# Gated delta rule on one core: the decay buffers doubled, the decay differences moved ahead in VectorE's order, and half of the block copies sent from ScalarE's queue

## The chip, the cores and the metric

The kernel runs on one core of one Trainium2 chip. The metric is the device time of one execution in microseconds (us). Three runs of the kernel before gave 2969.79 to 2971.79 us, with a median of 2971.08 us.

## The reference, cut to what matters

The model is two transformer-like blocks over 528 tokens (16 meta tokens and 512 others) with 1024 channels. Everything up to the delta rule and everything after it is unchanged by this edit; the edit lies in one stage of the first block, the gated delta rule, which is computed once forwards and once backwards in time for 8 heads of 128 channels.

```python
kk   = einsum("bnhid,bnhjd->bnhij", k, k)
decay = exp(where(tri, g[..., :, None] - g[..., None, :], -inf))
lmat = where(strict, beta[..., :, None] * kk * decay, 0.0)
a    = lmat + eye(CHUNK)
sol  = triangular_solve(a, concat(v * beta, k * beta * exp(g)))   # unit lower triangular
qk   = einsum("bnhid,bnhjd->bnhij", q, k) * decay
# then over the chunks, in order:
v_new = u_c - w_c @ S
o_c   = qd_c @ S + qk_c @ v_new
S     = S * exp(g_last) + kd_c.T @ v_new
```

Here `g` is the running sum of the log decays within a chunk, `qd` is q times exp(g), and S is the state that one chunk hands to the next. The outputs of both directions are added.

## The kernel before, in words

The stage cuts the 528 tokens into 5 chunks of C = 106 rows, and the 8 heads into 2 groups of 4. A step handles one chunk of 4 heads in both directions at once; there are STEPS = 10 steps. Direction u = 0 runs forwards and u = 1 backwards, and almost everything exists twice, once for each u. PSUM banks 0 to 3 belong to u = 0, and 4 to 7 to u = 1.

The order of the work is written out by hand, one function per engine: `pe_delta`, `act_delta`, `dve_delta`, `pool_delta` and `sp_delta`. Each has a loop over t that interleaves three steps in different phases. "Ahead" is step t: decays, k times k, and the inverses of the diagonal blocks. "Inner" is step t-1: the inverse is completed in three levels of matrix products. "Outer" is step t-2: solve, outputs and state. All engines run their own list in order, and wait on semaphores for what they need.

The pieces that the change touches or moves are these:

- `decay_diff(t)` on VectorE (DVE), L1423: differences of the summed decays, from the PSUM bank that TensorE (PE) filled in `spread_decay` (L1186), into the tile `dec`. ScalarE (ACT) takes their exponential in place in `exp_diff` (L1371).
- `decayed_qk(t-1)` on DVE, L1453: q times k times the previous step's `dec`, into `qkm`. Since there is one `dec` per direction, `decay_diff(t)` stands behind it, with a drain of DVE between them.
- `decayed_values(t-2)`, L1434, writes `rr`; PE's output products (`outputs`, L1263 and L1264) wait for it. `lower(t)`, L1444, then writes `mt`, the lower triangular matrix of the chunk.
- `exp_decay(t)` on ACT, L1366, writes `qd`, which has two buffers per direction; it waits until PE's outputs of step t-2 have read the buffer. GpSimd (POOL) multiplies it by q in L1314.
- `product_out` on ACT, L1376, copies a level's product from PSUM to `pp`. PE needs it for `level_update`, and DVE's `inverse_next` (L1474 and L1476) follows. The order on ACT is exp_diff, exp_decay, then product_out for levels 0, 1 and 2.
- The 16x16 diagonal blocks of `mt` are inverted on DVE (`block_begin`, L1494, and the functions after it). To bring 28 blocks of each direction into one layout, they go through DRAM: the sync engine's queue (SP) sends 7 small transfers for each direction into `block_in` (L1156, the "cuts"), waits until all 14 have landed, reads them back into `uu` and `raw` (L1159, L1160), later sends the inverted blocks out (L1163), and puts them into `xq` with 14 transfers (L1170, the "placements").
- DVE's order in one t is: rest, decayed_qk, drain, decay_diff, decayed_values, lower, add_output, inverse_next level 0, block_begin and the blocks up to size 4, state_next, inverse_next level 1, block 8 in two halves with inverse_next level 2 between them, block_turned.

After the last step SP goes on to load weights into `wraw` (L452), whose first half is the new room of one of the decay buffers.

Of the kernel before, what the change touches and what calls it, by code (L numbers as in the profile page):

```python
# [17 lines left out]
F32 = mybir.dt.float32  # L18
# [6 lines left out]
P = 128  # L25
# [125 lines left out]
def build_program(nc, io):  # L151
# [41 lines left out]
    eps = keep("eps", [P, 1])  # L193
    rstd = keep("rstd", [P, T])
# [37 lines left out]
    CB, PB = 4 * W4, 4 * GH * P  # L232
    free_h, free_l = stage_pos - 3 * 4 * DM, stage_pos - 4 * DM
    room = {"base": [base, base + KT * F], "b": [b_at, b_at + 2 * KT * F], "d": [d_at, nc.sbuf_usable_end],
            "stage": [stage_pos, stage_pos + 2 * F], "free_h": [free_h, free_h + 4 * DM],
            "free_l": [free_l, free_l + 4 * DM]}
# [11 lines left out]
    for u in range(2):  # L248
        d = {}
        d["kt"] = [dsb("base", f"kt{u}{v}", [C, GH * P]) for v in range(2)]  # L250
        d["vt"] = [dsb("b", f"vt{u}{v}", [C, GH * P]) for v in range(2)]
        d["state"] = dsb("base", f"state{u}", [P, GH * P])
        d["rr"] = dsb("stage", f"rr{u}", [C, GH * P])
        d["vn"] = dsb("d", f"vn{u}", [C, GH * P])
        d["xq"] = [dsb("b", f"xq{u}{v}", [C, 2 * W4]) for v in range(2)]
        d["qd"] = [dsb("d", f"qd{u}{v}", [P, W4]) for v in range(2)]
        d["qkm"] = [dsb("d", f"qkm{u}{v}", [C, W4]) for v in range(2)]
        d["mt"] = [dsb("b", f"mt{u}{v}", [C, W4]) for v in range(2)]
        d["dec"] = dsb("base", f"dec{u}", [C, W4])
# [114 lines left out]
    d_cut, d_in, d_y, d_yout = map(sem, ("blocks_cut", "blocks_in", "blocks_inverted", "blocks_out"))  # L374
# [767 lines left out]

    def sp_delta(sp):

        sp.wait_ge(d_y, 1)
        for u in range(2):
            sp.dma_start(scr_in[u], uu[0:LANES, :]).then_inc(d_cut, 16)
        sp.wait_ge(d_cut, 32)
        cells = [scr_in[u].rearrange("(r l) (a b) -> l a r b", l=NBLK, b=BASE) for u in range(2)]
        back = [scr_out[u].rearrange("w (r l) (a b) -> l a (w r) b", l=NBLK, b=BASE) for u in range(2)]  # L1150
        for n in range(STEPS):
            for u in range(2):
                sp.wait_ge(d_mt[u], n + 1)
                for bl in range(NBLK):
                    src, k = diagonal(delta[u]["mt"][n % 2], bl)
                    sp.dma_start(cells[u][bl, 0:k, :, 0:k], src).then_inc(d_cut, 16)  # L1156
            sp.wait_ge(d_cut, 32 + 32 * NBLK * (n + 1))
            sp.wait_ge(d_y, n + 1)
            sp.dma_start(uu[0:LANES, :], scr_in[0]).then_inc(d_in, 16)  # L1159
            sp.dma_start(raw[32:32 + LANES, :], scr_in[1]).then_inc(d_in, 16)  # L1160
            sp.wait_ge(d_y, n + 2)
            for u in range(2):
                sp.dma_start(scr_out[u].rearrange("w p n -> p w n"),  # L1163
                             yy[32 * u:32 * u + LANES, :].rearrange("p (w n) -> p w n", w=2)).then_inc(d_yout, 16)
            sp.wait_ge(d_yout, 32 * (n + 1))
            for u in range(2):
                sp.wait_ge(d_cleared[u], n + 1)
                for bl in range(NBLK):
                    dst, k = diagonal(delta[u]["xq"][n % 2], bl)
                    sp.dma_start(dst, back[u][bl, 0:k, :, 0:k]).then_inc(d_x0[u], 16)  # L1170

    def pe_delta(pe):
# [79 lines left out]
        def outputs(n, u):  # L1252
            d = delta[u]
            qd, qkm = d["qd"][n % 2], d["qkm"][n % 2]
# [47 lines left out]
    def pool_delta(pool):  # L1302
# [8 lines left out]
        def decay_q(n, u):  # L1311
            qd = heads4(delta[u]["qd"][n % 2], C)
            wait(pool, d_eg[u], n + 1)
            pool.tensor_tensor(qd, qd, columns4(n, u, 0), ALU.mult).then_inc(d_qd[u], 1)  # L1314
# [39 lines left out]
    def act_delta(act):  # L1354
# [8 lines left out]
        def exp_decay(n, u):  # L1363
            wait(act, d_darg[u], n + 1)
            wait(act, d_o[u], n - 1)
            act.activation(delta[u]["qd"][n % 2][:, :], ps[:, 4 * u + 2, 0:W4], ACT.Exp).then_inc(d_eg[u], 1)  # L1366

        def exp_diff(n, u):
            dec = delta[u]["dec"]
            wait(act, d_darg[u], n + 1)  # L1370
            act.activation(dec[:, :], dec[:, :], ACT.Exp).then_inc(d_dec[u], 1)  # L1371
# [19 lines left out]
        for t in range(STEPS + 2):  # L1391
# [4 lines left out]
            if t < STEPS:  # L1396
                each(exp_diff, t)
                each(exp_decay, t)
            if 1 <= t <= STEPS:
                for lv in range(L):  # L1400
                    each(product_out, t - 1, lv)

    def dve_delta(dve):
# [15 lines left out]
        def decay_diff(n, u):  # L1419
            d, cc, h = delta[u], chunk(n, u), head0(n)  # L1420
            wait(dve, d_gbc[u], n + 1)
            for r, sl in enumerate(head_slices(C)):
                last = dve.tensor_scalar(d["dec"][:, sl], ps[0:C, 4 * u + 2, sl],  # L1423
# [14 lines left out]
        def lower(n, u):  # L1438
# [4 lines left out]
            for r, sl in enumerate(head_slices(C)):  # L1443
                last = dve.scalar_tensor_tensor(d["mt"][n % 2][:, sl], ps[0:C, 4 * u + 1, sl],  # L1444
                                                tok_b[:, cc, h + r:h + r + 1], d["dec"][:, sl],
# [3 lines left out]
        def decayed_qk(n, u):  # L1449
# [3 lines left out]
            dve.tensor_tensor(d["qkm"][n % 2][:, :], ps[0:C, 4 * u, 0:W4], d["dec"][:, :], ALU.mult  # L1453
# [1384 lines left out]
```

## Time and profile before

| what | value |
|---|---|
| median of 3 runs | 2971.08 us |
| the profiled execution's own time | 2974.84 us |
| its span | 2973.1 us |
| PE busy | 2763.3 us (93%) |
| DVE busy | 1459.4 us (49%) |
| the delta rule's stretch | about 255 to 641 us |
| granted clock of PE over the span | 0.967 of full speed |

The span is what the trace covers. Shares over the whole span say little here, since the edit concerns the stretch of the delta rule alone. In a timeline row the number in brackets is the engine's idle time just before the row, and what ended it; "x8" means that eight instructions of one line were merged into the row. Starts are us from the start of the span. In a row of busy times the stretch comes first and then its length, and then what the group's line names.

### The profile page before, as it was taken

What the parts mean: (1) busy time and instruction counts of PE and PEld (TensorE: products, weight loads), DVE (VectorE), ACT (ScalarE), POOL (GpSimd) and SP (SyncE); (2) the same over time, 40 slices, a digit from 0 to 9 for tenths busy, and PEclk for the clock granted to TensorE, in tenths of its full rate; (3) what the DMA queues carried; (4) which work ended last, traced back from release to release, by engine and by line L of the source; (5) the groups of instructions that cost most, each with busy time, mean ns of one, the idle gap of its engine ahead of it and who ended that gap; (6) DMA issues with size and microseconds to landing.
All of it is one profiled execution on the core that took longest, in us unless ns stands there. A gap on an engine that the chain in (4) does not pass through costs nothing.

```text
span 2973.1 us, 48213 instructions
## 1 busy us (share of the span) xinstructions
PE 2763.3 (93%) x17591; PEld 2419.9 (81%) x17591; DVE 1459.4 (49%) x2316; ACT 1024.3 (34%) x1759; POOL 1096.7 (37%) x588
## 2 busy tenths in 40 slices
PE   6986888889999999999899789999999999999998
PEld 6964777868987778888679679999998988877876
DVE  2664676643221754233778555444366224555433
ACT  4761222223234242222423564222233255422221
POOL 3422333314434444444437103444443310244443
PEclk8997888889999999999999999999999999999999
DMA  2210000012233333333312002223322210123332
GB/s 95 91 49 7 10 10 10 10 40 85 92 92 92 92 94 92 97 94 92 92 43 65 8 1 68 88 88 90 92 85 79 66 35 1 57 85 99 92 92 92
DMA packets 88859, 197.90 MB, mean 67 GB/s; under 512 B 38140, under 2 KB 40238, under 8 KB 88728
## 3 DMA queue, kind: packets, MB, share of 16 engines
q1 hardware_dynamic: 84964, 192.72, 21.9%
q10 hardware_dynamic: 3764, 3.38, 0.4%
q8 instruction: 88, 1.44, 0.2%
q14 instruction: 43, 0.35, 0.0%
HBM read 192.24 MB, written 3.82 MB: 66 GB/s over the span
## 4 chain that ended last, share of the span: by engine, by line
issue 44%; PE 17%; POOL 12%; DVE 4%; ACT 1%; DVEq 1%; POOLq 1%; ACTq 0%
POOL wl L476 12%; PE ps L512 9%; PE ps L2151 2%; PE ps L2182 2%; DVE work L2051 1%; DVE top L2048 1%; PE ps L2169 1%; PE ps L1798 1%; PE ps L2301 1%; PE ps L2310 1%; ACT prob L2220 0%; POOLq L129 0%; DVE rowmax L2251 0%; PE ps L2154 0%; PE ps L887 0%
## 5 line engine op out<-in xcount | busy, mean ns | idle before, releaser
L476 POOL TENSOR_TENSOR wl<-wraw,wh 128x1024 fp32r<-128x1024 f32 x353 | 875.8, 2481 | 1293.0 <-ACT wh L468 1292.9
L468 ACT ACTIVATE wh<-wraw 128x1024 fp32r<-128x1024 f32 x353 | 372.5, 1055 | 578.4 <-PE ps L512 490.4
L512 PE MATMUL ps<-xah,wh 128*128 128x264 f32 (+1 forms) x2672 | 500.7, 328 | 23.4 <-ACT xah L841 14.2
L512 PE MATMUL ps<-xah,wl 128*128 128x264 f32 (+1 forms) x2672 | 488.3, 323 | 0.0
L512 PE MATMUL ps<-xal,wh 128*128 128x264 f32 (+1 forms) x2672 | 487.3, 322 | 0.0
L512 PEld LDWEIGHTS ps<-xah,wh 128*128 128x128 f32 x2672 | 406.0, 190 | 77.9 <-issue 23.4
L512 PEld LDWEIGHTS ps<-xah,wl 128*128 128x128 f32 x2672 | 403.9, 189 | 41.1 <-issue 0.5
L512 PEld LDWEIGHTS ps<-xal,wh 128*128 128x128 f32 x2672 | 402.8, 188 | 40.7
L660 DVE TENSOR_TENSOR res<-res,stage 128x512 f32 (+3 forms) x112 | 81.8, 730 | 440.1 <-ACT stage L576 440.1
L512 PE MATMUL ps<-xbh,wh 128*128 128x264 f32 (+1 forms) x1392 | 274.7, 337 | 13.4 <-POOL wl L476 12.8
L512 PE MATMUL ps<-xbh,wl 128*128 128x264 f32 (+1 forms) x1392 | 269.9, 334 | 0.0
L512 PE MATMUL ps<-xbl,wh 128*128 128x264 f32 (+1 forms) x1392 | 269.5, 333 | 0.0
L512 PEld LDWEIGHTS ps<-xbh,wh 128*128 128x128 f32 x1392 | 218.2, 189 | 48.1 <-POOL wl L476 16.4
L576 ACT ACTIVATE stage<-ps 128x512 f32<-128x512 f32 (+1 forms) x136 | 81.9, 602 | 467.3 <-PE ps L512 467.2
L512 PEld LDWEIGHTS ps<-xbh,wl 128*128 128x128 f32 x1392 | 217.9, 188 | 27.5
L512 PEld LDWEIGHTS ps<-xbl,wh 128*128 128x128 f32 x1392 | 217.5, 188 | 27.4
L653 DVE TENSOR_SCALAR xbh<-stage 128x512 f32 (+3 forms) x102 | 144.8, 1420 | 18.2 <-issue 16.6
L2151 PE MATMUL ps<-pf,qz 128*104 128x264 f32 (+4 forms) x384 | 124.0, 409 | 24.7 <-ACT prob L2220 13.8
L2251 DVE TENSOR_REDUCE rowmax<-ps 106x1 f32<-106x106 f32 (+4 forms) x160 | 77.7, 488 | 126.5 <-PE ps L2156 70.8
L655 DVE TENSOR_TENSOR xbl<-stage,xbh 128x512 f32 (+3 forms) x102 | 114.1, 1119 | 15.3 <-issue 1.3
L1178 PE MATMUL ps<-xq,ob 106*106 106x106 f32 x480 | 67.4, 309 | 51.7 <-DVE xq L1474 33.5
L1178 PEld LDWEIGHTS ps<-xq,ob 106*106 106x106 f32 x480 | 63.1, 221 | 53.6 <-DVE xq L1474 35.0
(332 smaller groups left out, 3277.7 us busy)
## 6 DMA issues: line engine op xcount, KB each, us to landing
wraw<-in_w SPq DMA_DIRECT2D x353, 512.0 KB, 3.5
res<-in_x SPq DMA_DIRECT2D x4, 528.0 KB, 5.5
res<-in_x ACTq DMA_DIRECT2D x1, 2048.0 KB, 7.8
out<-res SPq DMA_DIRECT2D x1, 2048.0 KB, 6.9
block_in<-mt SPq DMA_DIRECT2D x120, 4.0 KB
xq<-block_out SPq DMA_DIRECT2D x120, 8.0 KB
block_out<-yy SPq DMA_DIRECT2D x20, 56.0 KB
cossin<-in_cossin ACTq DMA_DIRECT2D x1, 528.0 KB
```

The source lines that it names most:

```text
L468: act.activation(wh[:, s * DM:(s + 1) * DM], wraw[:, s * DM:(s + 1) * DM], ACT.Copy).then_inc(hi_done, 1)
L476: pool.tensor_tensor(wl[:, s * DM:(s + 1) * DM], wraw[:, s * DM:(s + 1) * DM], wh[:, s * DM:(s + 1) * DM].bitcast(F32), ALU.subtract).then ...
L512: mm = pe.matmul(ps[:, 2 * s + h, 0:width], ws[:, s * DM + kk * P:s * DM + (kk + 1) * P], x[:, at:at + width], start=(h not in [o[0] for o ...
L576: act.activation(shaped(out(j, u), live), acc(b, live=live), func, **more).then_inc(acc_free, 1)
L653: dve.tensor_scalar(hi, x, 1.0, None, ALU.mult)
L655: return dve.tensor_tensor(lo, x, hi.bitcast(F32), ALU.subtract)
L660: return dve.tensor_tensor(r, r, live_stage(u) if live else stage_at(u), ALU.add)
L1178: mm = pe.matmul(out_[:, sl], lhs(r, sl), rhs(r, sl), start=True, stop=True)
L1798: mm = pe.matmul(ps[0:ROWS[t], 4 + 2 * (n % 2) + x, 0:c], ix_zero[:, 2 * (m % 2) + hh, C * t:ENDS[t]], pf[:, 16 * T + o:16 * T + o + c], s ...
L2151: pe.matmul(s, qz[:, 2 * (p % 2) + hh, t * C:ENDS[t]], pf[:, key + o:key + o + c], start=True, stop=False)
L2182: mm = pe.matmul(ps[0:rows, 7, t * 64:(t + 1) * 64], ptr[n % 2][0:ROWS[kb], kb * rows:(kb + 1) * rows], v[0:ROWS[kb], kb, col:col + 64], s ...
L2251: most = dve.tensor_reduce(m, psum_cols(plan["unit", n][0], rows, w_), AX.X if w_ <= 512 else AX.XY, ALU.max, negate=True)
```

## The change

Five edits go together. The tile `dec` gets two buffers per direction, used by n % 2. The tile `qd` gets three, used by n % 3, so that `exp_decay` waits for the outputs of step t-3 and not t-2. On DVE, `decay_diff(t)` is moved ahead of `decayed_qk(t-1)`, and the drain between them goes. The cuts of direction 1 are issued from ACT's queue, behind exp_decay and ahead of product_out. SP issues only those of direction 0, and waits for each direction by its own semaphore before it reads that direction back. Some small tiles change places (`uu`, `raw`), and SP waits at the end until the last `dec` has been read, since one buffer lies in the room for weights.

```diff
-        d["qd"] = [dsb("d", f"qd{u}{v}", [P, W4]) for v in range(2)]
+        d["qd"] = [dsb(("d", "d", ("rstd", "free_h")[u])[v], f"qd{u}{v}", [P, W4]) for v in range(3)]
-        d["dec"] = dsb("base", f"dec{u}", [C, W4])
+        d["dec"] = [dsb(("base", "free_raw")[v], f"dec{u}{v}", [C, W4]) for v in range(2)]
...
+    def cut_blocks(q, n, u):
+
+        cells = scr_in[u].rearrange("(r l) (a b) -> l a r b", l=NBLK, b=BASE)
+        q.wait_ge(d_mt[u], n + 1)
+        for bl in range(NBLK):
+            src, k = diagonal(delta[u]["mt"][n % 2], bl)
+            q.dma_start(cells[bl, 0:k, :, 0:k], src).then_inc(d_cut[u], 16)
...
         for n in range(STEPS):
+            cut_blocks(sp, n, 0)
             for u in range(2):
-                sp.wait_ge(d_mt[u], n + 1)
-                for bl in range(NBLK):
-                    src, k = diagonal(delta[u]["mt"][n % 2], bl)
-                    sp.dma_start(cells[u][bl, 0:k, :, 0:k], src).then_inc(d_cut, 16)
-            sp.wait_ge(d_cut, 32 + 32 * NBLK * (n + 1))
-            sp.wait_ge(d_y, n + 1)
-            sp.dma_start(uu[0:LANES, :], scr_in[0]).then_inc(d_in, 16)
-            sp.dma_start(raw[32:32 + LANES, :], scr_in[1]).then_inc(d_in, 16)
+                sp.wait_ge(d_cut[u], 16 + 16 * NBLK * (n + 1))
+                sp.wait_ge(d_y, n + 1)
+                blocks_of = (uu[0:LANES, :], raw[32:32 + LANES, :])[u]
+                sp.dma_start(blocks_of, scr_in[u]).then_inc(d_in, 16)
...
+        for u in range(2):
+            sp.wait_ge(d_qkd[u], STEPS)
...
         def exp_decay(n, u):
             wait(act, d_darg[u], n + 1)
-            wait(act, d_o[u], n - 1)
-            act.activation(delta[u]["qd"][n % 2][:, :], ps[:, 4 * u + 2, 0:W4], ACT.Exp).then_inc(d_eg[u], 1)
+            wait(act, d_o[u], n - 2)
+            act.activation(delta[u]["qd"][n % 3][:, :], ps[:, 4 * u + 2, 0:W4], ACT.Exp).then_inc(d_eg[u], 1)
...
                 each(exp_diff, t)
                 each(exp_decay, t)
+                act.wait_ge(d_cut[1], 16)
+                wait(act, d_in, 32 * t)
+                cut_blocks(act, t, 1)
...
             if outer:
                 each(rest, t - 2)
+            if ahead:
+                each(decay_diff, t)
             if inner:
                 each(decayed_qk, t - 1)
-            if ahead:
-                dve.drain()
-                each(decay_diff, t)
             if outer:
                 each(decayed_values, t - 2)
```

On DVE, in loop turn t = 4, the kernel before has this order (the numbers behind a tile's name tell buffers apart; rr is the rest and then the decayed values, mt the lower matrix):

```order
198 L1414 SCALAR_TENSOR_TENSOR rr_107<-ps,tok_neg,vt_104 106x128 x4
199 L1414 SCALAR_TENSOR_TENSOR rr_124<-ps,tok_neg,vt_121 106x128 x4
200 L1453 TENSOR_TENSOR qkm_114<-ps,dec_117 106x424
201 L1453 TENSOR_TENSOR qkm_131<-ps,dec_134 106x424
202 L1423 TENSOR_SCALAR dec_117<-ps,tok_cum 106x106 x4
203 L1423 TENSOR_SCALAR dec_134<-ps,tok_cum 106x106 x4
204 L1434 TENSOR_SCALAR rr_107<-ps,tok_bk 106x128 x4
205 L1434 TENSOR_SCALAR rr_124<-ps,tok_bk 106x128 x4
```

And the changed kernel, at the same place:

```order
198 L1427 SCALAR_TENSOR_TENSOR rr_107<-ps,tok_neg,vt_104 106x128 x4
199 L1427 SCALAR_TENSOR_TENSOR rr_126<-ps,tok_neg,vt_123 106x128 x4
200 L1436 TENSOR_SCALAR dec_118<-ps,tok_cum 106x106 x4
201 L1436 TENSOR_SCALAR dec_137<-ps,tok_cum 106x106 x4
202 L1466 TENSOR_TENSOR qkm_115<-ps,dec_119 106x424
203 L1466 TENSOR_TENSOR qkm_134<-ps,dec_138 106x424
204 L1447 TENSOR_SCALAR rr_107<-ps,tok_bk 106x128 x4
205 L1447 TENSOR_SCALAR rr_126<-ps,tok_bk 106x128 x4
```

The eight differences have moved ahead of the two qkm products, and write another buffer than the one that the products read. Row numbers are places in DVE's list; lines of the changed kernel are 13 higher here.

On ACT, a loop turn of the kernel before reads as follows, from the new values to level 1:

```order
121 L1383 ACTIVATE vn_108<-ps,tok_b 106x128 x4
122 L1383 ACTIVATE vn_125<-ps,tok_b 106x128 x4
123 L1371 ACTIVATE dec_117<-dec_117 106x424
124 L1371 ACTIVATE dec_134<-dec_134 106x424
125 L1366 ACTIVATE qd_111<-ps 128x424
126 L1366 ACTIVATE qd_128<-ps 128x424
127 L1376 ACTIVATE pp_118<-ps 106x424
128 L1376 ACTIVATE pp_135<-ps 106x424
```

In the changed kernel, a loop turn reads:

```order
161 L1393 ACTIVATE vn_108<-ps,tok_b 106x128 x4
162 L1393 ACTIVATE vn_127<-ps,tok_b 106x128 x4
163 L1381 ACTIVATE dec_118<-dec_118 106x424
164 L1381 ACTIVATE dec_137<-dec_137 106x424
165 L1376 ACTIVATE qd_112<-ps 128x424
166 L1376 ACTIVATE qd_131<-ps 128x424
167 L1152 DMA block_in<-mt_135 16x4x16 x6
168 L1152 DMA block_in<-mt_135 10x4x10
169 L1386 ACTIVATE pp_120<-ps 106x424
170 L1386 ACTIVATE pp_139<-ps 106x424
```

Seven transfers now stand between exp_decay and the first product_out.

## Rows read from the trace of the kernel before

**Rows 1.** PE, PEld, DVE, ACT, POOL busy (instructions), PE clock, DMA share, GB/s.

```profile
255.00:641.00 386.00, 313.50 (x2504) 296.20 (x2504) 251.81 (x714) 94.95 (x220) 130.85 (x140) 0.86 0.07 11
```

**Rows 2.** Waits of DVE, 255 to 641 us: total, times, longest.

```profile
DVE qkm L1453 <- PE ps L1178: 25.2, 9, 3.3
DVE uu L1494 <- DMA raw<-block_in: 21.8, 9, 7.8
```

**Rows 3.** Timeline of DVE in loop turn t = 5.

```profile
427.63 1.35 DVE L1453 TENSOR_TENSOR qkm<-ps,dec 106x424 f32<-106x424 f32 x2 [2.75 <-PE ps L1178]
429.07 1.98 DVE L1423 TENSOR_SCALAR dec<-ps,tok_cum 106x106 f32<-106x106 f32 x8
430.96 2.15 DVE L1434 TENSOR_SCALAR rr<-ps,tok_bk 106x128 f32<-106x128 f32 x8
433.03 1.97 DVE L1444 SCALAR_TENSOR_TENSOR mt<-ps,tok_b,dec 106x106 f32<-106x106 f32 x8
442.28 0.60 DVE L1476 TENSOR_TENSOR xq<-xq,ps 106x424 f32<-106x424 f32 x1
444.18 0.37 DVE L1494 COPY uu<-raw 28x256 f32<-28x256 f32 x1 [1.30 <-DMA raw<-block_in]
```

**Rows 4.** Timeline of DVE in t = 10, where no differences are due.

```profile
610.23 1.34 DVE L1453 TENSOR_TENSOR qkm<-ps,dec 106x424 f32<-106x424 f32 x2 [2.02 <-PE ps L1178]
611.49 2.15 DVE L1434 TENSOR_SCALAR rr<-ps,tok_bk 106x128 f32<-106x128 f32 x8
```

**Rows 5.** Timeline of SP's queue in t = 5.

```profile
434.09 7.03 SPq L1156 DMA_DIRECT2D block_in<-mt  x14
442.42 0.40 SPq L1160 DMA_DIRECT2D raw<-block_in  x1
```

**Rows 6.** Transfers issued from ACT's queue at the kernel's start.

```profile
0.76 0.44 ACTq L2551 DMA_DIRECT2D gains<-in_gains  x1
5.50 1.40 ACTq L2553 DMA_DIRECT2D sel<-in_sel  x1
```

**Rows 7.** ACT's first product_out of t = 2, 5 and 8.

```profile
322.12 0.52 ACT L1376 ACTIVATE pp<-ps 106x424 f32<-106x424 f32 x1 [0.85 <-PE ps L1178]
...
438.43 0.52 ACT L1376 ACTIVATE pp<-ps 106x424 f32<-106x424 f32 x1 [0.16 <-PE ps L1178]
...
546.28 0.52 ACT L1376 ACTIVATE pp<-ps 106x424 f32<-106x424 f32 x1 [0.16 <-PE ps L1178]
```

**Rows 8.** DVE's lower in t = 2, 6 and 8, block copy in 6 and 8.

```profile
319.00 1.97 DVE L1444 SCALAR_TENSOR_TENSOR mt<-ps,tok_b,dec 106x106 f32<-106x106 f32 x8
...
468.68 1.97 DVE L1444 SCALAR_TENSOR_TENSOR mt<-ps,tok_b,dec 106x106 f32<-106x106 f32 x8
...
478.93 0.67 DVE L1494 COPY uu<-raw 28x256 f32<-28x256 f32 x1 [2.58 <-DMA raw<-block_in]
...
539.35 1.97 DVE L1444 SCALAR_TENSOR_TENSOR mt<-ps,tok_b,dec 106x106 f32<-106x106 f32 x8
...
550.83 0.37 DVE L1494 COPY uu<-raw 28x256 f32<-28x256 f32 x1
```

**Rows 9.** PE's first output products in t = 5 and t = 6.

```profile
432.23 0.44 PE L1263 MATMUL ps<-qd,state 128*128 128x106 f32 x2 [2.40 <-DVE rr L1434]
...
467.39 0.39 PE L1263 MATMUL ps<-qd,state 128*128 128x106 f32 x2
```

**Rows 10.** Busy times in t = 5 and t = 6 beside these products.

```profile
432.50:435.50 3.00, 3.00 (x17) 3.00 (x16) 2.50 (x11) 0.00 (x0) 1.20 (x2) 0.51 0.04 7
467.50:470.50 3.00, 3.00 (x29) 3.00 (x28) 3.00 (x14) 1.64 (x3) 3.00 (x4) 1.00 0.16 17
```

**Rows 11.** One block product on DVE at t = 0 and t = 4, and POOL beside the latter.

```profile
272.61 0.43 DVE L1512 TENSOR_TENSOR tmp<-uu,yy 60x64 f32<-60x64 f32 x2
...
409.73 1.26 DVE L1512 TENSOR_TENSOR tmp<-uu,yy 60x64 f32<-60x64 f32 x2
409.08 1.79 POOL L1307 TENSOR_TENSOR mt<-scum,sel 16x424 f32<-16x424 f32 x2
```

More of the change, by code:

```diff
@@ L193, in build_program @@
     eps = keep("eps", [P, 1])
+    rstd_at = keep.pos[0]
     rstd = keep("rstd", [P, T])
@@ L255, in build_program @@
         d["xq"] = [dsb("b", f"xq{u}{v}", [C, 2 * W4]) for v in range(2)]
-        d["qd"] = [dsb("d", f"qd{u}{v}", [P, W4]) for v in range(2)]
+        d["qd"] = [dsb(("d", "d", ("rstd", "free_h")[u])[v], f"qd{u}{v}", [P, W4]) for v in range(3)]
         d["qkm"] = [dsb("d", f"qkm{u}{v}", [C, W4]) for v in range(2)]
         d["mt"] = [dsb("b", f"mt{u}{v}", [C, W4]) for v in range(2)]
-        d["dec"] = dsb("base", f"dec{u}", [C, W4])
+        d["dec"] = [dsb(("base", "free_raw")[v], f"dec{u}{v}", [C, W4]) for v in range(2)]
         d["pp"] = dsb("b", f"pp{u}", [C, W4])
         delta.append(d)
-    uu, raw, yy = (dsb("free_h", name, [64, n * BASE * BASE]) for name, n in (("uu", 1), ("raw", 1), ("yy", 2)))
+    uu, yy = dsb("base", "uu", [64, BASE * BASE]), dsb("free_h", "yy", [64, 2 * BASE * BASE])
+    raw = place("raw", [64, BASE * BASE], F32, room["free_l"][0])
     tmp, half = dsb("free_l", "tmp", [64, 2 * BASE * BASE]), dsb("free_l", "half", [64, BASE * BASE // 4])
@@ L373, in build_program @@
     d_cleared = both("inverse_cleared")
-    d_cut, d_in, d_y, d_yout = map(sem, ("blocks_cut", "blocks_in", "blocks_inverted", "blocks_out"))
+    d_cut = both("blocks_cut")
+    d_in, d_y, d_yout = map(sem, ("blocks_in", "blocks_inverted", "blocks_out"))
     d_ks, d_rr, d_xr, d_vn, d_vk, d_o, d_oa, d_ds, d_st = map(both, (
@@ L1170, in sp_delta @@
                     sp.dma_start(dst, back[u][bl, 0:k, :, 0:k]).then_inc(d_x0[u], 16)
+        for u in range(2):
+            sp.wait_ge(d_qkd[u], STEPS)
     def pe_delta(pe):
@@ L1253, in outputs @@
             d = delta[u]
-            qd, qkm = d["qd"][n % 2], d["qkm"][n % 2]
+            qd, qkm = d["qd"][n % 3], d["qkm"][n % 2]
             wait(pe, d_qd[u], n + 1)
@@ L1311, in decay_q @@
         def decay_q(n, u):
-            qd = heads4(delta[u]["qd"][n % 2], C)
+            qd = heads4(delta[u]["qd"][n % 3], C)
             wait(pool, d_eg[u], n + 1)
@@ L1422, in decay_diff @@
             for r, sl in enumerate(head_slices(C)):
-                last = dve.tensor_scalar(d["dec"][:, sl], ps[0:C, 4 * u + 2, sl],
+                last = dve.tensor_scalar(d["dec"][n % 2][:, sl], ps[0:C, 4 * u + 2, sl],
                                          tok_cum[:, u, cc, h + r:h + r + 1], 0.0, ALU.subtract, ALU.min)
@@ L1452, in decayed_qk @@
             wait(dve, d_o[u], n - 1)
-            dve.tensor_tensor(d["qkm"][n % 2][:, :], ps[0:C, 4 * u, 0:W4], d["dec"][:, :], ALU.mult
+            dve.tensor_tensor(d["qkm"][n % 2][:, :], ps[0:C, 4 * u, 0:W4], d["dec"][n % 2][:, :], ALU.mult
                               ).then_inc(d_qkd[u], 1)
```

15 lines of the change are left out of this document (7 added, 8 removed).

## The prediction

> **What bounds the kernel now.** First read the busy times by stretch: the edit lies in the 386.00 us of the delta rule, where PE is busy 313.50 us and DVE 251.81 [rows 1]. Neither is full, so here a cycle of waits sets the pace. The second view is DVE's waits. Two of them are those that the edit aims at: 25.2 us in front of qkm for PE's products, and 21.8 us in front of the block inversion for the blocks on their way through DRAM [rows 2]. The third view is the timeline of one loop turn. In t = 5 DVE idles 2.75 us before L1453, although the decay differences that come right behind it need only a PSUM bank filled before the solve; they take 1.98 us and delay the decayed values, which PE's outputs wait for, and `lower` [rows 3]. PE stands idle 2.40 us for those values [rows 9]. From `lower`'s start, called L (433.03), it goes on two ways that meet at the block copy: DVE's own level-0 updates end at 442.88 = L+9.85, and the blocks arrive at 444.18 = L+11.15, after 1.30 us of idling [rows 3]. From the block copy to the next `lower`, DVE's list has hardly a gap except the one before qkm. A turn takes some 37 us, and what is saved in one is saved in the time, since DVE's list runs through all of them.
>
> **Part 1: differences first.** Before, qkm to decayed values is 430.96 - 427.63 = 3.33 us start to start [rows 3]. At t = 10, where no differences are due, the same distance is 611.49 - 610.23 = 1.26 us [rows 4]. The difference, 2.07 us, goes from the path, provided the eight differences fit in the idle time before qkm. That is 2.75 us here against 1.98 us of work [rows 3]. The nine waits before qkm total 25.2 us; one of them is t = 10 with 2.02 [rows 2, 4], so the eight of t = 2 to 9 average 2.9 us. At t = 1 there is none and nothing is gained. 8 x 2.07 = 16.6 us. Next in line is POOL's masking of qkm, about 1 us for each direction behind the product, which ends before PE's second half of the outputs; I add nothing for it.
>
> **Part 2: the cuts from two queues.** SP issues 14 cuts in 7.03 us, and `raw` is issued 442.42 - 441.12 = 1.30 us after that [rows 5]. In the new order SP sends 7 from L+1.06, and ACT 7 from L+1.97, when the second `mt` is ready. An issue on ACT's queue held it 0.44 us at the start of the kernel [rows 6], about 0.47 with its spacing, so ACT's last ends near L+5.3; `raw` would be issued at about L+6.6 and be in SBUF 1.76 us later (444.18 - 442.42 [rows 3, 5]), at L+8.4. The blocks are then no longer late: DVE's level-0 updates are, at L+9.85. So each wait in front of the block copy can be won down to the 0.1 us that separates any two DVE instructions here, but no further.
>
> What hides ACT's seven issues? They stand ahead of product_out, which in t = 5 starts at 438.43 = L+5.40 [rows 7]: just the time at which the issues end (L+5.3). The cover is full with 0.1 us to spare. In t = 2 it is not: product_out starts at 322.12 = L+3.12, L being 319.00, so it would be pushed by 2.2 us; PE does both directions' products before the first update, which forgives 0.6, and 1.6 us are lost [rows 7, 8]. exp_decay, which stood before product_out and waited for the outputs, is out of the way, but PE had product_out's input hardly earlier, so I count nothing for the third `qd` buffer.
>
> The sum of part 2: waits of 21.8 us, of which the longest, 7.8, is t = 0, leave 14.0 us in eight turns of t = 1 to 9; t = 8 has none [rows 2, 8]. Off go 8 x 0.1 = 0.8, the 1.6 of t = 2, some 0.3 for smaller pushes of product_out, and 2.2 at t = 6. There no decayed values are due, so PE's outputs start at 467.39, before `lower` at 468.68 [rows 8, 9]: the updates don't get earlier with `lower`, and part 1 and part 2 together can win only the 2.58 us of idling there less 0.3, not 2.1 + 2.5. That leaves 9.1 us. At t = 0 nothing but the transfers is due: the last issue from ACT ends 1.9 us before SP's did, which is 1.9 us. Together 11.0 us.
>
> **Part 3: PE's clock.** In t = 5 PE comes out of 2.40 us of idling [rows 9], and from 432.50 to 435.50 its granted clock is 0.51, the lower of the two levels (1.2 and 2.4 GHz), with 17 products in 3 us; in t = 6 it comes straight from other products, the clock is 1.00, and 29 products fit in 3 us [rows 10]. After part 1 only 0.4 us of that idling are left, so the outputs may stay fast. 17 products at the fast pace take 17 x 3/29 = 1.76 us and not 3.00, so the 3 us hold at least 1.2 us of loss, about 1.6 with the slow rest on both sides of them. This would bring PE to level 0 some 1.6 us earlier, but ACT's issues until L+5.3 hold product_out, so I count it only where product_out was later than that: t = 8, with 546.28 = L+6.93, gives 1.3 us of the possible 1.6 [rows 7, 8]. Bounds: 0 (the clock falls as before) and 1.6 in that turn.
>
> **Part 4: DVE beside POOL.** The same two block products take 0.43 us at t = 0, and 1.26 at t = 4, where POOL's L1307 runs beside them [rows 11]. POOL's instructions of this place follow PE's level 1, which does not start earlier relative to L; the block work does, by up to 1.3 us, so more of it is done before POOL comes. One such row shows 0.8 us of loss per turn: the bounds are a gain of 0.8 x 9 = 7 us and, if the work only meets another of POOL's instructions, a loss of as much. I take 1.6 us of gain, twice the loss of that row, since POOL stands idle where the work moves to.
>
> The Trainium skill (page "SBUF — State Buffer", section "Who interferes with whom") says that a VectorE instruction with two SBUF inputs and a GpSimd instruction that reads SBUF exclude each other for a whole instruction, and the first to issue wins. This row agrees. It makes the sign of this term a matter of which comes first, and I leave it small.
>
> SP's new wait at the end holds the next weights back until the last qkm, which ends at 611.57 [rows 4], some 30 us before the stretch ends at 641; SP is then still at its placements, and I count nothing. Its bound is nothing too, since nobody needs those weights before 641.
>
> **Sum.** 16.6 + 11.0 + 1.3 + 1.6 = 30.5 us. The profiled execution took 2974.84 us, so it would be 2944.3; its span is 2973.1. The median of the runs is 3.8 us lower, 2971.08, which gives 2940.6. I forecast 2941.
>
> **The rivals.**
> - *Only part 1 counts.* The seven issues on ACT go slower than 0.47 us because both queues issue at once, or the transfers themselves, not their issue, take the time. For it: 7.03 us over 14 is 0.50, somewhat more than ACT's 0.47. Against it: the last cut lands 1.30 us after its issue, so at most a small part of the 8.3 us is transfer [rows 5]. If ACT needs 0.66 us an issue, product_out starts 1.3 us later, and the win of part 2 is gone. Gain 16.6 us or somewhat more with t = 0: 2953.
>  The Trainium skill (page "DMA: Bandwidth & Descriptors", section "Issuing engines are not separate DMA queues") says that transfers issued from several engines run on the same 16 DMA engines, and that a second issuer saves only issue time, usually little beside the transfer. By that rule this is the case to expect; the trace has the issue as the larger part, and I follow the trace.
> - *More than forecast.* Parts 3 and 4 at their upper ends (7 us for POOL, some 4 for a faster PE in all turns): 41 us, 2930. ACT's list speaks against it, since product_out can't be before L+5.3.
> - *Slower: ACT's queue becomes the bound.* With y us an issue, product_out starts at L+2.0+7y, and the updates end 4.45 us later (442.88 - 438.43 [rows 3, 7]). Before, the block copy stood at L+11.15. Part 1 gives 2.07, so the turn breaks even at 6.45 + 7y = 13.2, y = 0.97 us. ACT's longest issue at the start held it 1.40 us, though the usual one was 0.44 [rows 6]. At 1.40 a turn loses 3.0 us, eight turns 24: 2995.
> - *It doesn't do what it says*: the differences still wait, because PE's spread products come too late (they follow the transposes). Then they delay qkm and the gain of part 1 falls by up to 2 us a turn, leaving part 2: 2960. In t = 5 the bank is filled before the solve's products, over 2 us ahead of qkm, which speaks against it.
>
> **How the numbers follow.** Forecast 0.6 (2941, own range 2935 to 2947); only part 1 0.17; more than forecast 0.1; not as it says 0.04; slower 0.04; a mix that cancels within the noise 0.05. The range 2930 to 2956 takes in the first three. What a measurement of this kernel can tell from no change is about 0.2%, 5.9 us, or anything from 2965.1 to 2977.0. Faster 0.91, same 0.05, slower 0.04.
>
> **What would show it.** Part 1: the differences stand before qkm, with less than 1 us of idling left there, and qkm to decayed values is 1.3 us. Part 2: ACT's seven issues take 3.3 us and end at L+5.3, `raw` is issued before L+7.5, and the wait before the block copy is at most 0.2 us in most turns. If product_out starts behind the issues by more than a few tenths, ACT is the new bound. Part 3: a clock of 1.00 during the output products of all turns. Part 4: the stretch from block copy to state_next shorter than before. The forecast is wrong if a turn is shortened by less than 2.5 us, or if time after 641 us moves.

## The result, and the profile after

The changed kernel takes 2957.76 us (median of 8 runs, 2951.48 to 2965.11), the kernel before beside it 2972.18 us. The ratio is 0.9949, with a 95% interval from 0.9937 to 0.996: faster by 0.5%, some 15 us, half of the 30 forecast and just outside the range. The profiled execution took 2955.78 us, with a span of 2954.0.

Of the two stretches of a loop turn, one came as forecast and one did not. The page and answers of the changed kernel show it. First the busy times of the delta stage (columns as in [rows 1]) and the waits in it (total, times, longest):

```profile
255.00:625.00 370.00, 307.73 (x2513) 286.14 (x2514) 254.68 (x714) 92.39 (x223) 129.87 (x139) 0.90 0.09 15
```

```profile
ACT pp L1386 <- DMA block_in<-mt: 50.9, 8, 7.2
...
PE ps L1188 <- ACT pp L1386: 14.7, 7, 3.0
...
DVE qkm L1466 <- PE ps L1188: 10.4, 9, 2.0
...
DVE uu L1507 <- DMA raw<-block_in: 6.0, 1, 6.0
```

Both waits that the edit aimed at went: 25.2 us before qkm became 10.4, and of the 21.8 before the block copy only t = 0 is left [rows 2]. A new pair stands above them: ACT's product_out behind its own transfers, and PE behind product_out. Next the timeline of DVE in t = 5, answering to [rows 3]:

```profile
414.15 1.96 DVE L1436 TENSOR_SCALAR dec<-ps,tok_cum 106x106 f32<-106x106 f32 x8
416.96 1.35 DVE L1466 TENSOR_TENSOR qkm<-ps,dec 106x424 f32<-106x424 f32 x2 [0.85 <-PE ps L1188]
418.22 2.15 DVE L1447 TENSOR_SCALAR rr<-ps,tok_bk 106x128 f32<-106x128 f32 x8
420.29 1.97 DVE L1457 SCALAR_TENSOR_TENSOR mt<-ps,tok_b,dec 106x106 f32<-106x106 f32 x8
...
428.06 0.60 DVE L1487 TENSOR_TENSOR xq<-xq,ps 106x424 f32<-106x424 f32 x1 [4.15 <-PE ps L1188]
429.00 0.60 DVE L1489 TENSOR_TENSOR xq<-xq,ps 106x424 f32<-106x424 f32 x1 [0.34 <-PE ps L1188]
430.44 0.60 DVE L1487 TENSOR_TENSOR xq<-xq,ps 106x424 f32<-106x424 f32 x1 [0.84 <-PE ps L1188]
431.88 0.60 DVE L1489 TENSOR_TENSOR xq<-xq,ps 106x424 f32<-106x424 f32 x1 [0.84 <-PE ps L1188]
432.50 0.37 DVE L1507 COPY uu<-raw 28x256 f32<-28x256 f32 x1
```

The differences fill DVE's old gap, and qkm to decayed values is 1.26 us, as said. But `lower` to block copy is 12.21 us here, where it was 11.15 before and 9.95 was forecast. The four updates come late, and the last ones 1.44 us apart. What is ahead of them shows in the queues of ACT and SP (answering to [rows 5] and [rows 7]) and on PE:

```profile
422.37 3.99 ACTq L1152 DMA_DIRECT2D block_in<-mt  x7
426.45 0.94 ACT L1386 ACTIVATE pp<-ps 106x424 f32<-106x424 f32 x2 [7.22 <-DMA block_in<-mt]
```

```profile
421.35 4.02 SPq L1152 DMA_DIRECT2D block_in<-mt  x7
...
427.29 0.32 SPq L1168 DMA_DIRECT2D raw<-block_in  x1
```

```profile
422.89 0.39 PE L1274 MATMUL ps<-qkm,vn 106*128 106x106 f32 x2
423.12 1.66 PE L1188 MATMUL ps<-xq,ob 106*106 106x106 f32 x16
427.03 0.99 PE L1188 MATMUL ps<-pp,xq 106*106 106x106 f32 x8 [2.26 <-ACT pp L1386]
427.86 1.10 PE L1188 MATMUL ps<-xq,pp 106*106 106x106 f32 x8
428.75 1.65 PE L1188 MATMUL ps<-pp,xq 106*106 106x106 f32 x8
```

```profile
420.50:422.50 2.00, 2.00 (x20) 2.00 (x20) 1.91 (x9) 0.00 (x0) 2.00 (x4) 1.00 0.09 8
...
428.00:431.50 3.50, 3.50 (x25) 3.50 (x24) 1.79 (x3) 0.00 (x0) 0.00 (x0) 0.56 0.03 8
```

With the old idling gone, PE's clock is 1.00 through the outputs (it was 0.51 [rows 10]) and PE has level 0's products at 424.8. It then idles 2.26 us for ACT, whose seven issues took 3.99 us and not 3.3. Read one by one, six of them took 0.31 to 0.46 us, as forecast, and one took 1.32. SP had such a held issue at the same time, and both came free within 0.02 us of each other:

```profile
423.19 1.32 ACTq L1152 DMA_DIRECT2D block_in<-mt  x1
```

```profile
423.10 1.39 SPq L1152 DMA_DIRECT2D block_in<-mt  x1
```

Behind PE's idling the clock falls to 0.56, and a group of updates takes 1.65 us. In the kernel before, the same group took 0.91:

```profile
440.58 0.91 PE L1178 MATMUL ps<-pp,xq 106*106 106x106 f32 x8
```

So in this turn the idle time and the slow clock were not removed, but moved from before the outputs to before the updates. Over the whole stretch the clock still rose, from 0.86 [rows 1] to 0.90, since it fell before the updates only in t = 2, 5 and 7. The length of the idling doesn't tell which turns these are: PE idled 1.55, 2.26 and 2.97 us in them, and 1.39, 2.14, 2.14 and 2.27 us in t = 3, 4, 8 and 9, where the updates ran at 1.00. What else decides is not shown.

Last, a block product of t = 4 with POOL beside it, answering to [rows 11]:

```profile
397.41 2.06 DVE L1525 TENSOR_TENSOR tmp<-uu,yy 60x64 f32<-60x64 f32 x2
```

```profile
397.33 2.01 POOL L1331 TENSOR_TENSOR ob<-mt,masks 106x424 f32<-106x424 f32 x2 [5.72 <-PE ps L1188]
```

It took 1.26 us before, and takes 2.06 now: the earlier block copy leads it right under POOL's level-2 masks.

### The profile page after: what moved, and what is told of

It is laid out like the page before. It is cut to its first block, busy times and chain, and to the rows that moved or that the text cites. A ratio compares the mean times of both kernels' runs of the same rounds, so it can differ in the third digit from the quotient of the medians.

```text
span 2954.0 us, 48222 instructions
## 1 busy us (share of the span) xinstructions
PE 2755.0 (93%) x17591; PEld 2408.6 (82%) x17591; DVE 1461.9 (49%) x2316; ACT 1021.2 (35%) x1759; POOL 1096.8 (37%) x588
## 3 DMA queue, kind: packets, MB, share of 16 engines
q8 instruction: 88, 1.44, 0.2%
## 4 chain that ended last, share of the span: by engine, by line
issue 44%; PE 17%; POOL 12%; DVE 4%; ACT 1%; DVEq 1%; POOLq 1%; ACTq 0%
POOL wl L479 12%; PE ps L515 9%; PE ps L2163 2%; PE ps L2194 2%; DVE work L2063 1%; DVE top L2060 1%; PE ps L2181 1%; PE ps L1810 1%; PE ps L2313 1%; PE ps L2322 1%; ACT prob L2232 0%; POOLq L129 0%; DVE rowmax L2263 0%; PE ps L2166 0%; PE ps L890 0%
## 5 line engine op out<-in xcount | busy, mean ns | idle before, releaser
L515 PEld LDWEIGHTS ps<-xbh,wh 128*128 128x128 f32 x1392 | 218.1, 188 | 48.7 <-POOL wl L479 16.7
L656 DVE TENSOR_SCALAR xbh<-stage 128x512 f32 (+3 forms) x102 | 144.5, 1417 | 18.2 <-issue 16.6
L1386 ACT ACTIVATE pp<-ps 106x424 f32<-106x424 f32 x60 | 30.7, 523 | 195.4 <-PE ps L1188 137.0
L2242 ACT ACTIVATE ptr<-ps 106x106 f32<-106x106 f32 (+4 forms) x160 | 66.4, 416 | 85.9 <-PE ps L2181 85.9
```

The lines of the kernel that those rows point to most:

```text
L515: mm = pe.matmul(ps[:, 2 * s + h, 0:width], ws[:, s * DM + kk * P:s * DM + (kk + 1) * P], x[:, at:at + width], start=(h not in [o[0] for o ...
L656: dve.tensor_scalar(hi, x, 1.0, None, ALU.mult)
L1386: act.activation(delta[u]["pp"][:, :], ps[0:C, 4 * u, 0:W4], ACT.Copy).then_inc(d_ppc[u], 1)
L2242: last = act.activation(ptr[n % 2][:, 0:w_], ps[0:C, TURN_BANK[t], 0:w_], ACT.Copy)
```

## The experiments

All were timed in five rounds beside the kernel before. "Stage" is, in each trace, from the first `lower` to the clearing of `hinv` behind the stage. A is the ten distances from `lower` to block copy added up, B the nine from block copy to the next `lower`, and C the nine from block copy to the next instruction that isn't block work (t = 1 to 9; the first eight lie within B). All are in us and from starts in DVE's timeline.

| kernel | ratio (95%) | median | stage | A | B | C |
|---|---|---|---|---|---|---|
| before | 1 | 2972 to 2974 | 381.2 | 114.1 | 215.2 | 49.1 |
| changed | 0.9949 (0.9937-0.996) | 2957.76 | 360.5 | 110.4 | 199.6 | 52.8 |
| repeat | 0.9933 (0.992-0.9947) | 2953.64 | 364.4 | 113.0 | 199.8 | 53.6 |
| order only | 0.9943 (0.993-0.9955) | 2956.89 | 363.4 | 115.6 | 195.5 | 46.0 |
| queue only | 0.998 (0.9972-0.9989) | 2968.54 | 377.2 | 110.3 | 215.5 | 53.6 |
| ACT three | 0.9894 (0.9879-0.9909) | 2939.48 | 343.6 | 100.6 | 195.2 | 48.7 |
| ACT four | 0.9904 (0.9891-0.9918) | 2943.55 | 350.2 | 98.0 | 199.9 | 50.6 |
| PE busy | 0.9927 (0.9914-0.9941) | 2952.15 | 359.8 | 108.8 | 201.2 | 53.1 |
| two qd | 0.9986 (0.9977-0.9995) | 2967.35 | 373.5 | 126.6 | 197.2 | 52.3 |
| POOL narrow | 0.9873 (0.9858-0.9888) | 2934.08 | 343.4 | 115.0 | 181.3 | 41.9 |
| pp first | 0.993 (0.9918-0.9942) | 2952.01 | 357.1 | 109.7 | 197.8 | 49.6 |
| POOL late | 0.9847 (0.9834-0.986) | 2928.38 | 335.8 | 113.2 | 175.4 | 37.0 |
| three and late | 0.9819 (0.9806-0.9832) | 2922.35 | 333.0 | 102.5 | 179.4 | 36.9 |

**The changed kernel again.** No edit.

> The changed kernel once more, unaltered. The eight runs so far lie between 2951 and 2965 us, so this fixes how much a second set differs: theory, 14 to 19 us below the kernel before, and a delta stage (from the first lower to the clearing of hinv) of 360 us in the trace, against 381 before. Rival: the 21 us that the two traces show for the stage were luck of one execution, and this trace shows 15.

The ratio is 0.9933: 20 us below before, and 4 us better than the first set, slightly above what was expected. The two traces of the changed kernel differ by 4 us in the stage, 2.6 of it in A. The clock fell before the updates in four turns here (t = 2, 7, 8 and 9), and in three there. Differences of less than 4 us between medians are thus not read as effects below.

**All cuts back on SP.**

```diff
             cut_blocks(sp, n, 0)
+            cut_blocks(sp, n, 1)
...
-                act.wait_ge(d_cut[1], 16)
-                wait(act, d_in, 32 * t)
-                cut_blocks(act, t, 1)
```

> The changed kernel with all 14 cuts back on SP's queue; the early differences and the extra buffers stay. Theory (ACT's seven issues hold product_out, PE idles for it and then runs at the lower clock, so the second queue gives back most of what it wins): the wait before the block copy comes back at 1 to 2.5 us a turn, PE goes on without a pause, the stage takes 364 to 366 us, and the time is 3 to 5 us above the changed kernel's. Rival (the second queue still brings the 11 us forecast, and part 1 gave too little): stage 371 us or more, the time 10 us above the changed kernel's.

The time is that of the changed kernel within the intervals, so the second queue as built is worth nothing that can be told. DVE and ACT in t = 5:

```profile
421.36 1.97 DVE L1455 SCALAR_TENSOR_TENSOR mt<-ps,tok_b,dec 106x106 f32<-106x106 f32 x8
...
428.98 0.60 DVE L1487 TENSOR_TENSOR xq<-xq,ps 106x424 f32<-106x424 f32 x1 [0.15 <-PE ps L1189]
433.40 0.38 DVE L1505 COPY uu<-raw 28x256 f32<-28x256 f32 x1 [3.83 <-DMA raw<-block_in]
```

```profile
425.13 0.52 ACT L1387 ACTIVATE pp<-ps 106x424 f32<-106x424 f32 x1 [4.83 <-PE ps L1189]
```

Product_out starts at L+3.77 and the updates end at L+8.22, 3.83 us before the blocks are there. The loss in A against the changed kernel (5.2 and 2.6 us) comes back in B (4.1 and 4.3), and more than that in C: a later block copy meets less of POOL.

**Only the second queue.** DVE's order is put back, the drain too.

```diff
-            if ahead:
-                each(decay_diff, t)
             if inner:
                 each(decayed_qk, t - 1)
+            if ahead:
+                dve.drain()
+                each(decay_diff, t)
```

> The changed kernel with the decay differences back behind the products and the drain back in; half of the cuts stay on ACT's queue. Theory: here PE comes late to level 0 (its outputs run at the lower clock after the old idle time), so ACT's issues are mostly hidden behind it, and the second queue wins 0.5 to 1.4 us a turn: stage 370 to 373 us, time 8 to 11 us below before. Rival (an issue on ACT costs as much in any order): stage 377 to 380 us, time 1 to 4 us below before.

It wins 4 to 6 us (ratio 0.998): the rival's size. A is 3.8 us shorter, and C takes 4.5 us back, so the theory missed what the earlier copy runs into. The 50.9 us of waiting behind transfers on ACT are 29.6 us here, five times in place of eight, since PE often comes later than the issues end.

**Three cuts on ACT, four behind direction 0's on SP.** The new arguments of `cut_blocks` are the first cut to send and the one to stop before.

```diff
             cut_blocks(sp, n, 0)
+            cut_blocks(sp, n, 1, 3)
...
-                cut_blocks(act, t, 1)
+                cut_blocks(act, t, 1, 0, 3)
```

> The changed kernel with three of direction 1's cuts on ACT and four behind direction 0's on SP. Theory: ACT is free at about L+3.5 (L is the start of lower), when PE has the product, so PE doesn't idle and keeps the higher clock; the blocks land near L+9; block copy at about L+9 in most turns in place of L+10.5: stage 350 to 354 us, 7 to 10 us below the changed kernel. Rival (the late updates have another cause, such as the transfers or POOL): no better than the changed kernel, or slower by the later landing.

The time falls by 14 to 18 us against the changed kernel, to 2939.48, and A to 100.6. ACT, SP and DVE in t = 5:

```profile
418.38 1.26 ACTq L1152 DMA_DIRECT2D block_in<-mt  x3
420.07 0.52 ACT L1387 ACTIVATE pp<-ps 106x424 f32<-106x424 f32 x1 [4.83 <-DMA block_in<-mt]
```

```profile
417.35 5.43 SPq L1152 DMA_DIRECT2D block_in<-mt  x11
```

```profile
416.30 1.97 DVE L1458 SCALAR_TENSOR_TENSOR mt<-ps,tok_b,dec 106x106 f32<-106x106 f32 x8
...
425.23 0.37 DVE L1508 COPY uu<-raw 28x256 f32<-28x256 f32 x1 [0.72 <-DMA raw<-block_in]
```

Product_out is at L+3.77 and not delayed, the blocks wait 0.72 us, and `lower` to copy is 8.93 us. The theory holds: ACT's issues in front of product_out were the loss. Fewer issues are also held less often: one of ACT's was held in two turns (t = 8 and 9), and in five in the changed kernel. Against order only, whose cuts all stay on SP, A is 15.0 us shorter and the time 17 us.

**Four cuts on ACT.** As above with 4 in place of 3.

> As the kernel with three cuts of direction 1 on ACT, but with four: ACT is free at about L+3.9, 0.1 us after PE has the product, and SP ends one issue earlier. Theory (with three, the blocks' landing is the last again, by 0.7 to 2.5 us a turn): block copy 0.3 to 0.5 us earlier in most turns, time 2 to 5 us below the kernel with three. Rival (product_out behind the fourth issue costs as much): within 2 us of it.

A falls by another 2.6 us, but B grows by 4.7, and the time doesn't fall: 2943.55 against 2939.48, 4.1 us more, which is as much as two sets of one kernel differed by, and the intervals of the ratios overlap. The theory's gain of 2 to 5 us isn't there. The rival is nearer.

**PE kept busy.** Products that nobody reads fill PE's idle time before the first update.

```diff
+            if lv == 0 and u == 0 and 2 <= n + 1 < STEPS:
+                wait(pe, d_mt[u], n + 2)
+                for _ in range(3):
+                    products4(bank4(u, 1), lambda r, sl: column(n, u, 1, r), lambda r, sl: column(n, u, 1, r), C)
             wait(pe, d_ppc[u], L * n + lv + 1)
```

> The changed kernel, with three rounds of TensorE products that nobody reads put between level 0's products and its first update, into the bank that the update overwrites. They take about 2.2 us, the time that PE idles there for ACT. Theory (half of the loss is the clock that falls after that idling): the clock stays at 1.00 during the level-0 updates, they end about 4.4 us after product_out starts in every turn, the block copy stands at L+9.8 to L+10.7 in the turns where it stood above L+11, and the time is 4 to 10 us below the changed kernel's, although PE does more work. Rival (the clock has no part in it; ACT's lateness is all): no faster, or up to 3 us slower.

The busy times of t = 5 during the added products and the updates behind them (columns as in [rows 10]):

```profile
424.20:426.40 2.20, 2.20 (x27) 2.20 (x26) 0.00 (x0) 0.94 (x2) 2.20 (x3) 1.00 0.14 21
426.50:429.50 3.00, 3.00 (x35) 3.00 (x34) 1.78 (x3) 0.00 (x0) 0.18 (x1) 1.00 0.06 15
```

The clock stays at 1.00, so that half is shown: it was the idling that let it fall. The time is 2952.15, below both sets of the changed kernel but within 4 us of the nearer. The cleanest turn is t = 7: product_out starts at L+6.58 (L+6.50 in the changed kernel), and the block copy at L+11.05 in place of L+12.62, so the lower clock had cost about 1.6 us there. The added products cost something too: where the issues end early they are not done when product_out starts, and in t = 5 the block copy is 5.09 us behind product_out, where 4.47 is usual at the higher clock. As a cure it is worth little.

**Two qd buffers.**

```diff
...
-            wait(act, d_o[u], n - 2)
-            act.activation(delta[u]["qd"][n % 3][:, :], ps[:, 4 * u + 2, 0:W4], ACT.Exp).then_inc(d_eg[u], 1)
+            wait(act, d_o[u], n - 1)
+            act.activation(delta[u]["qd"][n % 2][:, :], ps[:, 4 * u + 2, 0:W4], ACT.Exp).then_inc(d_eg[u], 1)
```

> The changed kernel with two qd buffers again, so exp_decay waits for PE's outputs of the step two before, and ACT's issues stand behind it. Theory (the third buffer is worth something only because the issues stand behind exp_decay): PE's second half of the outputs ends near L+3, so the issues start at L+4 or later in place of L+2.1, product_out at L+7.5 or later, and the time is 10 to 18 us above the changed kernel's. Rival (as the prediction had it, the third buffer is worth nothing): within 3 us of the changed kernel.

It is 10 to 14 us slower than the changed kernel, as the theory said, with A at 126.6. The push in a turn was smaller than the theory had it: in most turns the issues start at L+3.2 and not L+4, and from t = 3 on product_out starts at L+6.4 to L+8.1. ACT in t = 4, where `lower` starts at 384.49:

```profile
387.57 0.52 ACT L1376 ACTIVATE qd<-ps 128x424 f32<-128x424 f32 x1 [1.26 <-PE ps L1274]
387.67 4.86 ACTq L1152 DMA_DIRECT2D block_in<-mt  x7
392.63 0.94 ACT L1386 ACTIVATE pp<-ps 106x424 f32<-106x424 f32 x2 [4.54 <-DMA uu<-block_in]
```

Here one issue was held for 2.09 us, the longest of all. The third buffer is what makes the second queue bearable at all; I had counted nothing for it.

**Product_out first.** ACT's seven issues behind level 0's product_outs.

```diff
-                act.wait_ge(d_cut[1], 16)
-                wait(act, d_in, 32 * t)
-                cut_blocks(act, t, 1)
             if 1 <= t <= STEPS:
-                for lv in range(L):
+                each(product_out, t - 1, 0)
+            if t < STEPS:
+                act.wait_ge(d_cut[1], 16)
+                wait(act, d_in, 32 * t)
+                cut_blocks(act, t, 1)
+            if 1 <= t <= STEPS:
+                for lv in range(1, L):
                     each(product_out, t - 1, lv)
```

> The changed kernel with ACT's seven issues behind level 0's two product_outs in place of ahead of them. Same queue, same transfers, another order. Theory (what the second queue costs is only product_out's lateness behind the issues): product_out starts at L+3.8 in most turns, PE neither waits nor slows, and the level-0 updates end near L+8.3; but direction 1's blocks are issued from L+4.9 to L+8.2 and arrive near L+11, which then sets the block copy. Stage 360 to 366 us, time within 3 us of the kernel with all cuts on SP. Rival (the second queue itself slows something, such as PE's waits or the placements): product_out at L+3.8, but the level-0 updates still end after L+9.8.

DVE in t = 4:

```profile
383.90 1.97 DVE L1460 SCALAR_TENSOR_TENSOR mt<-ps,tok_b,dec 106x106 f32<-106x106 f32 x8
...
391.52 0.59 DVE L1492 TENSOR_TENSOR xq<-xq,ps 106x424 f32<-106x424 f32 x1 [0.15 <-PE ps L1188]
394.42 0.94 DVE L1510 COPY uu<-raw 28x256 f32<-28x256 f32 x1 [2.30 <-DMA raw<-block_in]
```

The updates end at L+8.21, and the blocks come at L+10.52. With the same transfers from the same queue neither PE nor the clock suffers, which rules out that the queue itself is the harm. The stage is 357.1 us, a little under the band, and the time 2952.01, which is 4.9 us below order only, where at most 3 were expected.

**POOL's level-2 masks narrowed.** One head of four.

```diff
+            g = 1 if lv == 2 else GH
-            pool.tensor_tensor(heads4(d["ob"], C), heads4(d["mt"][n % 2], C),
-                               masks[:, u, lv, :].unsqueeze(1).broadcast_to([C, GH, C]), ALU.mult
+            pool.tensor_tensor(heads4(d["ob"], C)[:, 0:g, :], heads4(d["mt"][n % 2], C)[:, 0:g, :],
+                               masks[:, u, lv, :].unsqueeze(1).broadcast_to([C, g, C]), ALU.mult
```

> The changed kernel, with GpSimd's level-2 mask computed for one head of four: three quarters of that product are left out, so the result is another. Theory (DVE's block products wait for whole instructions of POOL, and the level-2 masks are the ones they meet): the stretch from the block copy to the state update falls from 5.5 to 6.2 us to 4.2 to 5 us, and the time is 6 to 12 us below the changed kernel's. Rival (the long block products come from decay_rows or from something else): the stretch changes by less than 0.5 us a turn, time within 3 us.

The time is 20 to 24 us below the changed kernel, more than expected, with C down by 11 us. Since work is left out and the result is another, this only shows where to look. In t = 4 the product beside the narrow masks takes 0.64 us in place of 2.06, and the next one now meets decay_rows:

```profile
390.75 0.64 DVE L1526 TENSOR_TENSOR tmp<-uu,yy 60x64 f32<-60x64 f32 x2
...
391.83 1.83 DVE L1544 TENSOR_TENSOR tmp<-yy,half 60x64 f32<-60x64 f32 x2
```

```profile
391.76 1.77 POOL L1317 TENSOR_TENSOR mt<-scum,sel 16x424 f32<-16x424 f32 x2
```

**POOL's level-2 masks held.** Nothing is left out; they wait until DVE's first state update.

```diff
                 each(masked, t - 1, 1)
+                if 2 <= t < STEPS and not last_chunk(t - 2):
+                    wait(pool, d_st[0], updates(t - 2) + 1)
                 each(masked, t - 1, 2)
```

> The changed kernel, with GpSimd's level-2 masks held until DVE's first state update of the turn is done, in the seven turns that have one; nothing is left out. Theory (DVE's block products with two SBUF operands wait for whole instructions of POOL): the stretch from block copy to state update falls from 5.5 to 6.2 us to 3.9 us or less in those seven turns, POOL's masks then run beside DVE's PSUM operations at no cost, and the time is 10 to 15 us below the changed kernel's. Rival (the masks held back delay PE's level 2 by as much as they give, or meet the 512-element block products): within 4 us of it, or slower.

2928.38 us: 25 to 29 us below the changed kernel, twice what was expected. POOL and DVE in t = 4:

```profile
391.06 1.98 POOL L1331 TENSOR_TENSOR ob<-mt,masks 106x424 f32<-106x424 f32 x2 [10.40 <-DVE state L1569]
```

```profile
388.22 0.44 DVE L1527 TENSOR_TENSOR tmp<-uu,yy 60x64 f32<-60x64 f32 x2
...
389.88 2.14 DVE L1569 SCALAR_TENSOR_TENSOR state<-state,chunk_decay,ps 128x128 f32<-128x128 f32 x8
```

The block stretch is 3.7 us in six of the seven turns and 3.93 in the last, and the state update beside the masks still takes 2.14. Of the 24.2 us that B fell by, 14.5 are the block stretches in it. DVE's waits in B fell from 17.9 to 7.6 us in all (the one before qkm is 0.30 us in t = 5 in place of 0.85); why each of them shrank I did not separate. The rival was right in a small part: in four turns the first 512-element product now takes 1.50 us, and 1.02 in the changed kernel.

**Both together.** The edits of the two.

> Both together: three cuts of direction 1 on ACT, and the level-2 masks held. Theory (the two losses are independent: one lies before the block copy, one behind it): the gains of 16 and of 10 to 15 us add, time 2925 to 2932 us, stage 330 to 335 us. Rival (with both, SP's placements push the cuts, so part is lost): 2933 to 2940 us.

2922.35 us, ratio 0.9819: 1.8% under the kernel before, and better than both kernels of this study. It lies below both bands that were expected, since POOL late alone was worth more than had been put in. The two gains don't add in full: POOL late brings 17 us on top of three cuts, and 25 to 29 alone. One trace cannot say where the rest went; A and B are 2 and 4 us above the better of the two parents.

## Why the prediction was wrong, point by point

**Part 1** was right in mechanism and size. The bracket of 1.26 us from t = 10 [rows 4] came true in t = 2 to 5 and 7 to 9 to the hundredth. The idling left before qkm was 0.85 to 1.41 us, in half of the eight turns somewhat more than the 1 us named as its limit. B fell by 15.6 us against the 18.2 of parts 1 and 4. Without its block stretches it fell by 18.7, and by 16.2 in order only, where part 1 stands alone, against 16.6 forecast. So the shortfall is part 4's.

**Part 2** is the step that failed, at the sentence "The cover is full with 0.1 us to spare" and at the price of the issues, 3.3 us for seven. The cover was product_out's start at L+5.40 [rows 7], read from a turn in which PE ran at the lower clock. Part 3 said itself that this slowness would go, and then used the new, earlier PE only to cap a gain, not to ask what ACT's lateness does to a PE that now has to wait. Order only shows where product_out starts when no issue stands in front of it: from t = 2 on at L+3.77 in most turns, and at L+5.06 at the latest (t = 6). So the issues lay on the path in every one of these turns, not only in t = 2.

That alone doesn't change the sum, which had product_out at L+5.3 in any case. Two costs do. The first is the price of the issues, and it would have come under the old cover too. A plain issue cost what was forecast (0.45 us), but in five of the eight turns one of the seven was held for 1.2 to 1.6 us. The seven then took 3.9 to 4.3 us, and product_out stood 0.7 to 1.2 us behind L+5.3, 4.4 us in all. This was there to be read in the kernel before. The 7.03 us of [rows 5] have such an issue in them, and turns without one took 6.15 to 6.18:

```profile
434.43 1.14 SPq L1156 DMA_DIRECT2D block_in<-mt  x1
```

The second cost comes from the lost cover: PE's idling brought the lower clock back in t = 2, 5 and 7, where block copy minus product_out is 6.05 to 6.12 us and not 4.47: 1.6 us each, 4.8. The forecast had A at 114.1 - 12.3 = 101.8, the 12.3 being parts 2 and 3. The two costs, 9.2 us, cover the 8.6 up to the 110.4 measured, and the repeat (113.0) had more of both. With only three issues on ACT, A is 100.6 and the time 2939.48, against 2941 forecast; that these numbers meet is in part luck, for there the updates end earlier than the forecast had them, at L+8.2 in t = 5, and the blocks come last again. ACT's place in the path is shown by three experiments (three cuts, product_out first, order only), the clock's part by PE busy.

**Part 3** was right that the outputs would stay at the higher clock, and wrong in giving the clock a gain only: the idle time had moved.

**Part 4** had the wrong sign. I took POOL to be idle where the block work moves to. It is, for 1.9 us, and then the 64-element products meet the level-2 masks at their start: C grew by 3.7 us where a gain of 1.6 was forecast. The bounds held the value, but the row [rows 11] was read as the size of the whole effect. A stretch of 5.5 us on average, against 3.75 for the same work at t = 0, was there to be read: in t = 4 of the kernel before, two 16-element products beside the masks took 0.98 us, and 0.26 at t = 0. Holding the masks took the stretch to 3.7 us, and POOL late shows that to be worth more than all of part 2.

**The third qd buffer** was counted at nothing. As an edit beside the queue it is worth 10 to 14 us, since ACT's issues stand behind exp_decay.

**The sum.** The stage was to lose 30.5 us and lost 20.7 in the traces: 3.7 in A where 12.3 were forecast, 15.6 in B where 18.2 were, and 1.4 in the last turn behind its block copy, where none were. The span lost only 19.1, because the time after the stage was 2.2 us longer. The prediction had named that as a sign of being wrong; but over all 13 traces, whatever their edits, this time lies between 2331.5 us (before) and 2334.0, and POOL late has 2331.7, so no effect of the edit is shown in it. The medians differ by 14.4 us: the profiled execution of the kernel before was above its median, and that of the changed kernel below.

The rivals' 2953 ("Only part 1 counts") and 2960 ("It doesn't do what it says") lie close to the two sets (2957.76 and 2953.64), but neither by its mechanism. The differences didn't wait for their bank, as the rows of t = 5 show. ACT's issues were slow because single ones were held, which happened with one queue as well, and that was about half of the loss in A. Nor does the rule hold here that the first of the two rivals quoted from the Trainium skill (page "DMA: Bandwidth & Descriptors", section "Issuing engines are not separate DMA queues"), by which the issue time that a second queue saves is usually small: with three cuts on it, the second queue is worth 17 us.

## What to carry to other kernels

A wait read from a trace as cover belongs to the pace at which the engine before it ran. When one edit speeds that engine up, read the cover again before another edit hides work behind it. Transfers issued from a computing engine's queue are instructions of that engine: count them in front of whatever stands behind them, look at each issue and not at the mean, and give it only as many as end before its next input is there (three and not seven here). And where a small VectorE operation takes a whole multiple of its usual time, look for the GpSimd instruction beside it, and move that under VectorE operations that read PSUM.

## What the runs showed of the hardware that I had not expected

The issue of one small transfer took 0.43 us on SP's queue and 0.45 on ACT's in nearly every case, whether one queue was issuing or both. But about once in a loop turn, in all 13 traces, one issue was held for 0.7 to 2.1 us, mostly 1.1 to 1.8. With both queues issuing, it often hit both, and both came free together (t = 5: 1.39 and 1.32 us); in other turns it hit one alone (t = 9: ACT's seven took 4.00 us, SP's 3.06). It was there with a single queue too: 1.50 us in t = 4 and 1.14 in t = 5 of the kernel before, where the 14 took 6.15 to 7.5 us in all. What holds the issue stays open. VectorE products of 64 elements with two SBUF operands took 0.43 us for two, and up to 2.06 beside two GpSimd instructions of 1 us each, while VectorE's state update, with one operand in PSUM, took 2.14 us with and without them.
